# A gate's sigmoid computed as a tanh, and the gate inputs' loads moved from GpSimd's queue to SyncE's

## The chip, the cores and the metric

The kernel runs on one core of a Trainium2 chip. The metric is the device time of one execution in microseconds (us); the time before is 2019.53 us, the median of three runs (2018.4 to 2019.54). Lower is better.

## The reference

One layer of a streaming encoder is applied to a prompt of 1,024 frames and to 64 further frames of a running stream (1,088 tokens together), model width 2,048. An input projection gives the columns of two branches. The first, a state-space branch of width 1,024, ends in a gated linear unit (GLU), and this is the part that the change touches:

```
zs    = gelu(y_ssm)
y_ssm = zs * sigmoid(zs @ w_glu + b_glu)
y_ssm = y_ssm * silu(z_ssm)
y_ssm = rmsnorm(y_ssm, ssm_ng)
```

The second is an attention branch with 8 heads of width 128: q and k are RMS-normalised, forget gates are added to the logits, and then come a softmax, the product with v, and a SiLU gate. Both branches are normalised, concatenated, multiplied by `w_out` and added to the input. The outputs are the new frames, the new rows of k, v and the forget gates, and the final states.

## The kernel before

Everything is transposed: a tile has 128 features on the partitions and the 1,088 tokens along the free axis, in three blocks of 384, 384 and 320 columns (`COLS`), each block in a PSUM bank of its own (`GB`).

**The weight stream.** All large products run through the class `Weights`. A weight piece is two 128x128 tiles. SyncE loads it (`load`, L166, into one of four slots of `wraw`), ScalarE rounds it to its high part (`split_hi`, L171, `whi`), VectorE takes the rest (`split_lo`, L175, `wlo`), and TensorE multiplies (`multiply`, L187): 3 blocks x 2 tiles x 3 products = 18 matmuls. Piece m is split four pieces ahead of its use, into the slots of the piece m-4, which must have been multiplied; and SyncE may load piece m once piece m-4 has been split by VectorE. Each engine has one instruction stream, written out step by step; a step s is one piece.

**The stages.** A state-space stage comes first, and then eight attention heads (`part(h, True, ...)`, 32 pieces each). In the steps of head h lies also the softmax of head h-1. `part(None, False, True, NH - 1)` is the GLU stage: 32 pieces of `w_glu` in 8 panels of 4 pieces (`GP` is 4), and between them the softmax of the last head, in 9 row blocks. At the steps in `S_AT` (0, 3, 5, 7, 10, ...) logits are made, and ScalarE runs an Exp over them (L1522), which VectorE scales (L1726, tile `PR`). At the steps in `T_AT` (2, 4, 6, 8, 12, ...) TensorE transposes the result (L1986, L1989 for the 64-row block), behind the 18 matmuls of that step. At those in `O_AT` (3, 5, 7, ...) it multiplies with V (L1944). 128 pieces of `w_out` follow.

**One panel of the GLU.** When step 4n+3 is multiplied, ScalarE makes three Sigmoids from the three PSUM banks into `SG` (L1473), with the bias in a column of `vec`. The next panel's first matmuls wait for the bank they write. At the head of step 4n+4 VectorE runs `gate_glu(n)` (L1610): `SG` times `ZG` (L1614), then times `ZS` (L1616). ScalarE squares the product later in the same step (`square_glu`, L1435), behind `split_hi` and the step's copy of transposed rows, and VectorE adds the squares up (L1650, L1653). `SG`, `QG`, `ZG` are the buffers `QR`, `KR`, `VR` of the heads, and `ZS` lies in `KO`, the buffer from which the last head's k rows are stored.

**Table sets.** Some of ScalarE's functions need a table set that must be loaded first. `table(func)` (L1427) runs a one-column activation of that function, so that its set is loaded there: the trace shows an `ACT_TABLE_LOAD` and a small `ACTIVATE`. In the GLU stage `table(ACT.Sigmoid)` stands at the end of step 4n+2 (L1560), `table(ACT.Exp)` right behind the three Sigmoids (L1475).

**Who loads the gate inputs.** GpSimd, in its own stream (L1374 to L1381). For panel 0 it waits until the last head's v is transposed (`v_mm`) and its k rows are stored from `KO` (`k_out`); for the panels after, it waits for the product of the panel before (`yg`), stores it to `ys_s` (`finish_glu`, L1373), and loads `ZG` and `ZS` of the next. SyncE's stream in that stage has the weight pieces (`glu_piece`), the reload of the attention outputs (`load_ya`, L1284), and then the pieces of `w_out` with the reload of the gated products (`load_ys`, L1289).

Of the kernel before, what the change touches and what calls it, by code (L numbers as in the profile page):

```python
# [23 lines left out]
NH, HD = 8, 128  # L24
# [3 lines left out]
P = 128  # L28
# [8 lines left out]
RAW, SPL = 4, 4  # L37
# [13 lines left out]
def build_kernel(nc, x_prompt, x_sample, cache_k, cache_v, cache_logf, state_ssm_re, state_ssm_im,  # L51
# [66 lines left out]
    with ctx:  # L118
# [14 lines left out]
        def group(bank, b, p=slice(0, P)):  # L133

            return bank[p, 512 * b:512 * b + COLS[b][1]]

        def cols(a, b):

            return a[:, COLS[b][0]:COLS[b][0] + COLS[b][1]]
# [1012 lines left out]
        def attention(st, W, past):  # L1152
# [33 lines left out]
            stands = {}  # L1186
# [76 lines left out]
            def sync(sp, state_space):  # L1263
                def head(h, s):
                    col = h * P + 2 * D_SSM + D_ATT * (s // 8)
                    W.load(sp, h * NPC + s, s, col, PIECE * (s % 8))
                for s in range(NPC):
                    head(0, s)
                    state_space(s)
                with sp.Fori(1, NH) as h:  # L1270
                    for s in range(NPC):
                        head(h, s)

                def glu_piece(s):
                    W.load(sp, GLU0 + s, s, s // GP * P, PIECE * (s % GP), w_glu_v)

                def load_z(k):
                    sp.wait_ge(W.mm, W.multiplied(GLU0 - NPC // 4 + k // PIECE))
                    sp.dma_start(raw(XL[:, k]), zg_s[k * P:(k + 1) * P, :]).then_inc(zin[k], 16)

                def load_ya(k):
                    sp.wait_ge(W.mm, W.multiplied(GLU0 - NPC // 4 + (KG + k) // PIECE))
                    sp.wait_ge(e["y_out"], 16 * (k + 1))
                    sp.dma_start(raw(XL[:, KG + k]), ya_s[k * P:(k + 1) * P, :]).then_inc(yain[k], 16)  # L1284

                def load_ys(k):
                    sp.wait_ge(W.mm, W.multiplied(OUT0 - GP + k // PIECE))
                    sp.wait_ge(e["ys_out"], 16 * (k + 1))
                    sp.dma_start(raw(XL[:, k]), ys_s[k * P:(k + 1) * P, :]).then_inc(ysin[k], 16)  # L1289

                def out_load(n, s):
                    W.load(sp, out_piece(n, s), s, n * P, out_k(s), w_out_v, apart=s == HPC)
                for s in range(RAW):
                    glu_piece(s)
                    for k in range(PIECE * s, PIECE * (s + 1)):
                        load_z(k)
                for s in range(RAW, KG * GP):
                    glu_piece(s)
                    if s - RAW < KG - 1:
                        load_ya(s - RAW)  # L1300
                for s in range(NPO):
                    out_load(0, s)
                    if s >= HPC:
                        for k in range(PIECE * (s - HPC), min(PIECE * (s - HPC + 1), KG - 1)):
                            load_ys(k)
                with sp.Fori(1, NCH) as n:
                    for s in range(NPO):
                        out_load(n, s)
                stand(sp, "load")
                c = (NCH - 1) * P  # L1310
                for i in range(2):
                    sp.wait_ge(f["add"], stands["add"] + 2 * (NCH - 1) + i + 1)
                    sp.dma_start(y_prompt[0].rearrange("(m p) n -> p m n", p=P)[:, 4 * i:4 * i + 4, c:c + P], XO[1][:, 4 * i:4 * i + 4]
                                 ).then_inc(f["end_out"], 16)
                sp.wait_ge(f["add"], stands["add"] + 2 * (NCH - 1) + 3)
                sp.dma_start(y_sample[0][:, c:c + P], XO[1][0:DEC, TT - 1]).then_inc(f["end_out"], 16)
                sp.wait_ge(f["end_out"], 48)

            def gpsimd(pool):
# [52 lines left out]
                    pool.wait_ge(e["yg"], stands["yg"] + n + 1)  # L1372
                    pool.dma_start(ys_s[n * P:(n + 1) * P, :], SG[:]).then_inc(e["ys_out"], 16)  # L1373
                for n in range(KG):  # L1374
                    if n == 0:
                        pool.wait_ge(e["v_mm"], NH)
                        pool.wait_ge(e["k_out"], 32 * NH)
                    else:
                        finish_glu(n - 1)
                    pool.dma_start(ZG[:], zg_s[n * P:(n + 1) * P, :]).then_inc(e["zs_in"], 16)  # L1380
                    pool.dma_start(ZS, zs_s[n * P:(n + 1) * P, :]).then_inc(e["zs_in"], 16)  # L1381
                part(None, False, True, NH - 1)
                pool.wait_ge(e["v_out"], 32 * NH)

# [37 lines left out]
            def scalar(act, tail):  # L1422
# [35 lines left out]
                def part(h, gemm, att, ha):  # L1458
                    last = isinstance(h, int) and h == NH - 1
                    for s in range(NPC):  # L1460
# [3 lines left out]
                        if not gemm and s % GP == GP - 1:  # L1464
                            n = s // GP
                            if n:
                                act.wait_ge(e["ys_out"], 16 * n)
                            for b in range(3):
                                if b < 2:
                                    act.wait_ge(W.done[b], W.tiles + 4 * NH + n + 1)  # L1470
                                else:
                                    act.wait_ge(W.mm, W.multiplied(NH * NPC + s))
                                S.activation(cols(SG, b), group(GB, b), ACT.Sigmoid, bias=vec[:, 8 + n:9 + n]  # L1473
                                             ).then_inc(e["sig"], 1)
                            table(ACT.Exp)  # L1475
                        if gemm and s in (7, 15, 23):
                            raw = {7: QR, 15: KR, 23: VR}[s]
                            if s == 7 and att:
# [77 lines left out]
                            S.copy(KO[0:DEC, TT - 1], TB[0:DEC, 4 * 512:4 * 512 + P]).then_inc(e["k_act"], 1)  # L1556
                        if not gemm and s in YA_AT:
                            split_ya(YA_AT[s])
                        if not gemm and s % GP == GP - 2:
                            table(ACT.Sigmoid)  # L1560
                        if not gemm and s % GP == 0 and s:
                            square_glu(s // GP - 1)
                        if gemm and s == NPC - 2:
# [43 lines left out]
            def vector(dve, tail):  # L1607
                o = Order(dve, "dve_att")

                def gate_glu(n):  # L1610

                    dve.wait_ge(e["sig"], stands["sig"] + 3 * n + 3)
                    dve.wait_ge(e["zs_in"], 32 * (n + 1))
                    V.tensor_tensor(SG[:], SG[:], ZG[:], ALU.mult).then_inc(e["y1"], 1)  # L1614
                    dve.wait_ge(e["y1"], stands["y1"] + n + 1)
                    V.tensor_tensor(SG[:], SG[:], ZS, ALU.mult).then_inc(e["yg"], 1)  # L1616

                def gates(s):

# [49 lines left out]
                def part(h, gemm, att, ha):  # L1669
                    last = isinstance(h, int) and h == NH - 1  # L1670
                    for s in range(NPC):
# [11 lines left out]
                        if gemm:  # L1683
                            m = s + SPL
                            W.split_lo(h * NPC + m, m)
                            if not att:
                                tail(s)
                                if s == 6:
                                    state_space_over(dve)
                                    V.tensor_scalar(qg[:], vec[:, 32:33], HD ** -0.5, None, ALU.mult).then_inc(e["qg"], 1)  # L1690
                                    dve.wait_ge(e["qg"], 1)
                            if not att:
                                gates(s)
                        else:
                            W.split_lo(NH * NPC + s + SPL, s + SPL)
# [472 lines left out]
```

## Time and profile before

| what | value |
|---|---|
| median of three runs | 2019.53 us |
| the profiled execution's own time | 2019.47 us |
| its span | 2017.9 us |
| TensorE busy (matmuls) | 1965.8 us, 97% |
| VectorE busy | 1019.1 us, 51% |
| ScalarE busy | 681.3 us, 34% |
| GpSimd busy | 463.3 us, 23% |
| mean granted TensorE clock | 0.993 of full speed |
| mean DMA rate over the span | 89 GB/s |

The span runs from the first to the last instruction of the profiled execution. The time of an execution is a little longer: 1.6 us lie around the span. The matmuls are pipelined, so that the durations of two neighbours overlap; a busy share near 100% says that TensorE had always something to do, not that it was at its peak. Bracketed text at the end of a timeline row tells how long the engine was idle before it, and what released it.

### The profile page before, as it was taken

The page shows a single profiled execution, that of the slowest core. Times are in us where ns is not written, and L with a number is a line of the kernel's source. Part 1 is how long each engine was busy: PE and PEld are TensorE (multiplying, and loading weights), DVE is VectorE, ACT ScalarE, POOL GpSimd, SP SyncE. Part 2 cuts the span into 40 slices and gives each one's busy share as a digit, 9 for nine tenths or more (in the row PEclk, how much of TensorE's full clock was granted, in tenths as well). Part 3 has the DMA queues.
Part 4 walks back from the last instruction along what each step waited for, and adds up shares of the span by engine and source line. Part 5 has one row for each costly group of instructions (what it writes and reads, how often), then busy time and mean ns, then how long its engine had stood idle before and what let it go on. Part 6 is the DMA issues. An engine that isn't in the chain of part 4 may idle for free.

```text
span 2017.9 us, 35512 instructions
## 1 busy us (share of the span) xinstructions
PE 1965.8 (97%) x12368; PEld 1901.7 (94%) x12368; DVE 1019.1 (51%) x1984; ACT 681.3 (34%) x1368; POOL 463.3 (23%) x732
## 2 busy tenths in 40 slices
PE   5999999999999999999999999999989999999999
PEld 4799999999999999999999999999988999999998
DVE  7755666555453544635445354544655643333333
ACT  6422333333333343343333433343456631111110
POOL 5864444555110010010100001010020212222221
PEclk8999999999999999999999999999999999999999
DMA  8344444344322121131311213121273533333332
GB/s 226 95 107 109 108 111 104 104 115 129 86 57 62 35 82 37 34 85 31 84 34 45 73 34 84 34 78 39 82 254 132 201 93 86 86 86 86 88 86 65
DMA packets 220264, 179.91 MB, mean 89 GB/s; under 512 B 33090, under 2 KB 200156, under 8 KB 218996
## 3 DMA queue, kind: packets, MB, share of 16 engines
q1 hardware_dynamic: 200032, 117.39, 22.4%
q0 software_dynamic: 14656, 50.71, 8.1%
q10 hardware_dynamic: 5524, 11.14, 1.5%
q8 instruction: 30, 0.49, 0.1%
q14 instruction: 22, 0.18, 0.0%
HBM read 133.24 MB, written 45.93 MB: 89 GB/s over the span
## 4 chain that ended last, share of the span: by engine, by line
PE 89%; DVE 5%; ACT 2%; issue 2%; DMA 2%; SPq 0%; POOL 0%; DVEq 0%; ACTq 0%; POOLq 0%
PE GB L187 64%; PE TB L187 9%; PE TB L1944 3%; PE TB L1965 3%; PE TB L1986 2%; PE TB L1126 1%; PE TB L1136 1%; PE TB L1137 1%; PE TB L2005 1%; PE TB L2045 1%; PE TB L1032 1%; PE GB L1048 1%; DVE XL L668 1%; PE TB L1930 1%; ACT L1427 0%
## 5 line engine op out<-in xcount | busy, mean ns | idle before, releaser
L187 PE MATMUL GB<-XH,whi 128*128 128x384 f32 x2832 | 955.9, 338 | 10.3 <-DVE UP L744 5.1
L187 PE MATMUL GB<-XH,wlo 128*128 128x384 f32 x2832 | 926.6, 327 | 0.0
L187 PE MATMUL GB<-XL,whi 128*128 128x384 f32 x2832 | 923.7, 326 | 0.0
L175 DVE TENSOR_TENSOR wlo<-wraw,whi 128x256 fp32r<-128x256 f32 x540 | 269.8, 502 | 711.6 <-ACT whi L171 707.3
L187 PEld LDWEIGHTS GB<-XH,whi 128*128 128x128 f32 x2832 | 532.4, 188 | 26.2 <-issue 13.2
L187 PEld LDWEIGHTS GB<-XL,whi 128*128 128x128 f32 x2832 | 532.7, 188 | 5.3 <-issue 3.8
L171 ACT CAST whi<-wraw 128x256 fp32r<-128x256 f32 x540 | 218.3, 406 | 943.1 <-PE GB L187 785.2
L187 PEld LDWEIGHTS GB<-XH,wlo 128*128 128x128 f32 x2832 | 531.7, 188 | 0.0
L1341 POOL DMA_DIRECT2D ya_s<-ZR x7 | 4.1, 587 | 729.6 <-DVE ZR L1703 729.6
L1750 DVE RECIPROCAL SQ<-SQ 128x136 f32<-128x136 f32 x128 | 127.6, 997 | 1.1
L187 PE MATMUL TB<-XH,wlo 128*128 128x384 f32 (+1 forms) x384 | 125.8, 328 | 0.0
L187 PE MATMUL TB<-XH,whi 128*128 128x384 f32 (+1 forms) x384 | 125.5, 327 | 0.0
L187 PE MATMUL TB<-XL,whi 128*128 128x384 f32 (+1 forms) x384 | 125.5, 327 | 0.0
L1522 ACT ACTIVATE PR<-PR,nmx 128x128 f32<-128x128 f32 (+8 forms) x72 | 53.4, 742 | 186.5 <-DVE nmx L1721 173.3
L1427 ACT ACT_TABLE_LOAD x64 | 82.1, 1283 | 1.1
L1944 PE MATMUL TB<-PT,VT 128*128 128x128 f32 x576 | 74.7, 275 | 0.8 <-ACT PT L1532 0.8
L1944 PEld LDWEIGHTS TB<-PT,VT 128*128 128x128 f32 x576 | 71.3, 191 | 1.6 <-ACT PT L1532 1.3
L1965 PE MATMUL TB<-KN,QN 128*128 128x512 f32 (+2 forms) x192 | 72.4, 486 | 0.0
L187 PEld LDWEIGHTS TB<-XH,whi 128*128 128x128 f32 x384 | 72.1, 188 | 0.1
L187 PEld LDWEIGHTS TB<-XH,wlo 128*128 128x128 f32 x384 | 72.1, 188 | 0.0
L187 PEld LDWEIGHTS TB<-XL,whi 128*128 128x128 f32 x384 | 72.0, 188 | 0.0
L1716 DVE CUSTOM_DVE_ANT_0 PR<-TB,NCB 128x128 f32<-128x128 f32 (+3 forms) x64 | 41.0, 640 | 33.4 <-PE TB L1965 22.2
(389 smaller groups left out, 2060.3 us busy)
## 6 DMA issues: line engine op xcount, KB each, us to landing
wraw<-in_w_in SPq DMA_DIRECT2D x380, 128.0 KB, 2.2
wraw<-in_w_out SPq DMA_DIRECT2D x128, 128.0 KB, 2.2
xt<-in_x_prompt SPq DMA_DIRECT2D x5, 1024.0 KB, 5.5
NCB<-nc_s POOLq DMA_DIRECT2D x8, 608.0 KB, 5.2
us_s<-UP SPq DMA_DIRECT2D x8, 548.0 KB, 2.9
U<-us_s SPq DMA_DIRECT2D x64, 68.5 KB, 3.0
vs_s<-SS SPq DMA_DIRECT2D x8, 548.0 KB, 2.7
YT<-vs_s SPq DMA_DIRECT2D x64, 68.5 KB, 2.8
```

The costliest lines, as they stand in the source:

```text
L171: S.copy(whi[:, s % SPL], wraw[:, s % RAW]).then_inc(self.hi, 1)
L175: V.tensor_tensor(wlo[:, s % SPL], wraw[:, s % RAW], whi[:, s % SPL].bitcast(f32), ALU.subtract).then_inc(self.lo, 1)
L187: ins = T.matmul(group(GB if bank is None else bank, b), w[:, s % SPL, kk], x[:, k + kk, c:c + n], start=first and kk == 0 and i == 0, sto ...
L668: V.tensor_tensor(XL[:, 4 * b:4 * b + 4, m * P:m * P + n], tb, XH[:, 4 * b:4 * b + 4, m * P:m * P + n].bitcast(f32), ALU.subtract).then_in ...
L1032: ins = T.matmul(TB[0:2 * NH, 4 * 512:4 * 512 + n], wg[:, k], x[:, k, c:c + n], start=k == 0 and x is XH, stop=k == KT - 1 and x is XL)
L1427: o.then(S.activation(tabs[:], epsc[:], func))
L1522: S.activation(PR[0:n, 0:w], PR[0:n, 0:w], ACT.Exp, bias=nmx[0:n], accum_out=rsum[0:n]).then_inc(e["exp"], 1)
L1716: V.tensor_tensor_reduce(out=PR[0:n, 0:w - n], in0=TB[0:n, 0:w - n], in1=NCB[0:n, c:c + w - n], scale=1.0, scalar=-3e38, op0=ALU.add, op1= ...
L1750: o.then(V.reciprocal(a, a))
L1944: ins = T.matmul(O, VT[:, b], PT[:, b * P:(b + 1) * P], start=b == 0, stop=b == i)
L1965: ins = T.matmul(TB[:, c:c + cw], q, KN[:, c:c + cw], start=True, stop=True)
L1986: ins = T.transpose(TB[:, 1024 + b * P:1024 + (b + 1) * P], PR[:, b * P:(b + 1) * P], ident[:])
```

## The change

Five edits, which make one version:

1. ScalarE computes tanh((x + b)/2), in place of sigmoid(x + b), by `ACT.Tanh` with `scale=0.5`; VectorE makes up for it in the two products, as sigmoid(t) = 0.5 (1 + tanh(t/2)): (SG + 1) * ZG, then (SG * 0.5) * ZS. Both become `scalar_tensor_tensor`.
2. Eight columns of `vec` (the bias `b_glu`) are halved once by VectorE, in the first head. ScalarE waits for that before the first panel.
3. `table(ACT.Sigmoid)` and `table(ACT.Exp)` of the GLU stage are left out.
4. The loads of `ZG` and `ZS` are issued by SyncE (`load_gate(n)`) behind weight piece 8+4n of the GLU, and for n = 6 and 7 behind pieces 0 and 4 of `w_out`, where n = 7 stands ahead of the first `load_ys`. The waits are those that GpSimd had.
5. GpSimd keeps only the stores to `ys_s`. ScalarE gets a wait on `sqg`, its own squaring of the panel before.

```diff
@@ sync
+                def load_gate(n):
+                    if n == 0:
+                        sp.wait_ge(e["v_mm"], NH)
+                        sp.wait_ge(e["k_out"], 32 * NH)
+                    else:
+                        sp.wait_ge(e["yg"], stands["yg"] + n)
+                    sp.dma_start(ZG[:], zg_s[n * P:(n + 1) * P, :]).then_inc(e["zs_in"], 16)
+                    sp.dma_start(ZS, zs_s[n * P:(n + 1) * P, :]).then_inc(e["zs_in"], 16)
+                AHEAD = RAW + SPL
                 for s in range(RAW, KG * GP):
                     glu_piece(s)
                     if s - RAW < KG - 1:
                         load_ya(s - RAW)
+                    if s >= AHEAD and (s - AHEAD) % GP == 0:
+                        load_gate((s - AHEAD) // GP)
                 for s in range(NPO):
                     out_load(0, s)
+                    if s % GP == 0 and s // GP < AHEAD // GP:
+                        load_gate(KG - AHEAD // GP + s // GP)
                     if s >= HPC:
                         for k in range(PIECE * (s - HPC), min(PIECE * (s - HPC + 1), KG - 1)):
                             load_ys(k)
@@ gpsimd
                 for n in range(KG):
-                    if n == 0:
-                        pool.wait_ge(e["v_mm"], NH)
-                        pool.wait_ge(e["k_out"], 32 * NH)
-                    else:
+                    if n:
                         finish_glu(n - 1)
-                    pool.dma_start(ZG[:], zg_s[n * P:(n + 1) * P, :]).then_inc(e["zs_in"], 16)
-                    pool.dma_start(ZS, zs_s[n * P:(n + 1) * P, :]).then_inc(e["zs_in"], 16)
@@ scalar
                             if n:
                                 act.wait_ge(e["ys_out"], 16 * n)
+                                act.wait_ge(e["sqg"], stands["sqg"] + n)
+                            else:
+                                act.wait_ge(e["qg"], 2)
...
-                                S.activation(cols(SG, b), group(GB, b), ACT.Sigmoid, bias=vec[:, 8 + n:9 + n]
+                                S.activation(cols(SG, b), group(GB, b), ACT.Tanh, bias=vec[:, 8 + n:9 + n], scale=0.5
                                              ).then_inc(e["sig"], 1)
-                            table(ACT.Exp)
...
-                        if not gemm and s % GP == GP - 2:
-                            table(ACT.Sigmoid)
@@ vector
-                    V.tensor_tensor(SG[:], SG[:], ZG[:], ALU.mult).then_inc(e["y1"], 1)
+                    V.scalar_tensor_tensor(SG[:], SG[:], 1.0, ZG[:], ALU.add, ALU.mult).then_inc(e["y1"], 1)
                     dve.wait_ge(e["y1"], stands["y1"] + n + 1)
-                    V.tensor_tensor(SG[:], SG[:], ZS, ALU.mult).then_inc(e["yg"], 1)
+                    V.scalar_tensor_tensor(SG[:], SG[:], 0.5, ZS, ALU.mult, ALU.mult).then_inc(e["yg"], 1)
...
-                                    dve.wait_ge(e["qg"], 1)
+                                    V.tensor_scalar(vec[:, 8:16], vec[:, 8:16], 0.5, None, ALU.mult).then_inc(e["qg"], 1)
+                                    dve.wait_ge(e["qg"], 2)
```

## Rows read from the trace of the kernel before

**Rows 1.** The page's head, and the GLU stage as one stretch by engine

```profile
span 2017.9 us, 35512 instructions
...
core 0: us, PE busy (x) PEld busy (x) DVE busy (x) ACT busy (x) POOL busy (x), PEclk, DMA share, GB/s
1476.00:1606.00 130.00, 119.01 (x725) 112.89 (x724) 70.33 (x147) 77.37 (x137) 18.96 (x30) 1.00 0.51 173
```

**Rows 2.** TensorE's waits from 1475 to 1640 us: total, times, longest

```profile
PE TB L1986 <- DVE PR L1726: 5.2, 2, 3.1
PE GB L187 <- ACT QR L1473: 3.8, 4, 1.7
...
PE TB L1989 <- DVE PR L1726: 1.2, 1, 1.2
PE TB L1944 <- ACT PT L1532: 0.8, 2, 0.5
```

**Rows 3.** Timeline of TensorE, steps 4 and 6 of the GLU

```profile
1494.45 0.44 PE L1986 MATMUL TB<-ident,PR 128*128 128x128 f32 x2 [2.07 <-DVE PR L1726]
...
1505.18 0.55 PE L1986 MATMUL TB<-ident,PR 128*128 128x128 f32 x3 [3.15 <-DVE PR L1726]
```

**Rows 4.** Timeline of ScalarE, panels 0 and 2

```profile
1489.40 1.28 ACT L1427 ACT_TABLE_LOAD   x1
...
1490.93 0.41 ACT L171 CAST whi<-wraw 128x256 fp32r<-128x256 f32 x1
...
1499.61 1.12 ACT L1435 ACTIVATE KR<-QR 128x1088 f32<-128x1088 f32 x1 [4.31 <-DVE QR L1616]
1500.63 0.39 ACT L171 CAST whi<-wraw 128x256 fp32r<-128x256 f32 x1
...
1524.62 1.28 ACT L1427 ACT_TABLE_LOAD   x1
...
1526.14 1.47 ACT L1473 ACTIVATE QR<-GB,vec 128x384 f32<-128x384 f32 x3
```

**Rows 5.** Timeline of VectorE around the first gate product

```profile
1494.04 0.35 DVE L1726 TENSOR_SCALAR PR<-PR,rrec 128x256 f32<-128x256 f32 x1
1496.95 1.29 DVE L1614 TENSOR_TENSOR QR<-QR,VR 128x1088 f32<-128x1088 f32 x1 [2.56 <-DMA KO<-zs_s]
```

**Rows 6.** The chain that ended last, two of its pieces: start, us, what

```profile
1481.18 8.14 DMA out_k_sample<-KO
...
1490.50 6.35 DMA KO<-zs_s
```

**Rows 7.** Timeline of SyncE: weight pieces 8 and 9, and a reload

```profile
1480.51 0.38 SPq L166 DMA_DIRECT2D wraw<-in_w_glu  x1
1480.99 0.56 SPq L1284 DMA_DIRECT2D XL<-ya_s  x1
1483.70 0.38 SPq L166 DMA_DIRECT2D wraw<-in_w_glu  x1
```

**Rows 8.** Loads of 544 KB by SyncE (L1279) and by GpSimd (L1381): issue and landing

```profile
L1279 SPq DMA_DIRECT2D XL<-zg_s x8: 430/444/471, 1449.0 to 1466.4; - x8
...
DMA to landing us min/median/max: 3.9/4.6/6.2
...
L1381 POOL DMA_DIRECT2D KO<-zs_s x8: 531/531/543, 1490.5 to 1598.3; - x8
...
DMA to landing us min/median/max: 6.4/7.9/9.0
```

**Rows 9.** Groups by line from 1484 to 1612 us: busy us, mean ns of one

```profile
L1427 ACT ACT_TABLE_LOAD x16 | 20.5, 1283 | 0.3
...
L1614 DVE TENSOR_TENSOR QR<-QR,VR 128x1088 f32<-128x1088 f32 x8 | 10.3, 1284 | 2.6 <-DMA KO<-zs_s 2.6
L1661 DVE SCALAR_TENSOR_TENSOR XL<-XL,vec,XH 128x1088 fp32r<-128x1088 f32 x7 | 9.4, 1348 | 1.4 <-ACT XH L1444 1.4
```

**Rows 10.** Timeline of ScalarE in the first head: the loads at its Exp and its Ln

```profile
549.00 1.28 ACT L1503 ACT_TABLE_LOAD   x1
...
552.72 1.28 ACT L1506 ACT_TABLE_LOAD   x1
```

**Rows 11.** The first reloads of the gated product, and the split that reads them

```profile
1597.88 2.47 SPq L1289 DMA_DIRECT2D XL<-ys_s  x2
...
1609.52 2.29 ACT L1452 ACTIVATE XH<-XL,vec 128x1088 fp32r<-128x1088 f32 x2
```

## The prediction

> **What bounds the kernel now.** I read the page's head, then the GLU stage as one stretch, then TensorE's waits there, and last the timelines of the other engines around the two longest waits. TensorE is the bound: over the whole span it is nearly always busy, and in the GLU stage it is busy 119.01 of 130.00 us at a granted clock of 1.00 [rows 1]. The change adds and removes no matmul. All that it can give is therefore in the 11.0 us in which TensorE stood still there, and the waits account for them: 5.2 + 3.8 + 1.2 + 0.8 = 11.0 us [rows 2]. Two come from the softmax's normalised rows being late for a transpose (2.07 us at step 4, 3.15 us at step 6 [rows 3]), one of 1.2 us from the same at step 8, four (3.8 us) from a PSUM bank that the Sigmoid had not yet emptied, and two (0.8 us) from a late copy of transposed rows. The reader should ask of each: is ScalarE late because of a table load, or because of the gate inputs?
>
> **The table loads (edits 1 and 3).** 16 loads of 1283 ns stand in the stage [rows 9]. With its one-column activation each costs 1490.93 - 1489.40 = 1.53 us from its start to the next instruction [rows 4]; without it ScalarE still needs about 0.04 us to go on, so I take 1.5 us. 24 us of ScalarE's time go, but ScalarE is not the bound, and only what ends in a TensorE wait counts.
>
> - Step 4. Behind panel 0's Sigmoids ScalarE loads the Exp set, and only then splits a weight piece at 1490.93. VectorE's split, its logits, the Exp and the scaling follow, up to 1494.39 [rows 5], and the transpose at 1494.45. Without that load all of it comes 1.5 us earlier (the load ahead of the Sigmoids doesn't count here, since their last bank comes from TensorE). Wait 2.07 -> 0.57 us.
> - Step 8 is the same chain: 1.2 us of wait, 1.5 us of load gone, so the whole 1.17 us.
> - Bank waits. At panel 2 the load begins at 1524.62, right behind the Exp of step 10, and the Sigmoids at 1526.14 [rows 4]. Without the load they begin 1.5 us earlier, which leaves about 0.2 us of the longest wait (1.7 us). The other three are together 3.8 - 1.7 = 2.1 us, each under 1.5 us, and go whole. Gain 1.5 + 2.1 = 3.6 us.
> - The two late copies, 0.8 us, stand behind the Exp load of their panel, and go.
>
> Without step 6 this is 1.17 + 3.6 + 0.8 = 5.55 us behind step 6, and 1.5 us ahead of it.
>
> A row against a rule: the Trainium skill ("ScalarE: Activation LUTs", What ACT_TABLE_LOAD costs) gives a switch 1283 ns for the load and some 1380 ns of drain more, 2.66 us in all. Here the load and all that goes with it take 1.53 us [rows 4], so that the drain is not seen, and the row decides. By the page step 4's wait would have gone whole, which makes the sum about 0.5 us larger at most.
>
> **The gate loads (edit 4).** The wait at step 6 has another cause. After 1494.39 VectorE stands 2.56 us for `ZS` [rows 5], which landed 6.35 us after its issue at 1490.50; and that issue had waited for the store of the last k rows, out of the same buffer, until 1481.18 + 8.14 = 1489.32 [rows 6]. Behind the gate product are queued, on ScalarE, the squaring at 1499.61 and behind it the split at 1500.63 [rows 4], and from that the row block which TensorE waits for at 1505.18 [rows 3]. So step 6's transpose comes 1505.18 - 1496.95 = 8.23 us after the start of the gate product. Without the table load VectorE would arrive there at 1494.39 - 1.5 = 1492.9 us, and would wait for the load even longer. What the removed table load gives at step 4 is given back at step 6, unless the load lands earlier.
>
> The store that must end is the same, and the data ahead of it in the queues is nearly the same. SyncE is there in time: it issues piece 8 at 1480.51 and a reload at 1480.99 [rows 7], and would then stand at `load_gate(0)` from about 1481.6 until 1489.3. GpSimd's second load was issued 1490.50 - 1489.32 = 1.2 us after the store had landed; SyncE's, with 0.44 us for one [rows 8], about 0.5 us after, at 1489.8. SyncE's own loads of the same shape land in 4.6 us in the median (3.9 to 6.2), GpSimd's in 7.9 (6.4 to 9.0) [rows 8]. Of these I take 4.6: it landed at 1494.4, I say 1494.5. Bounds: 6.2 gives 1496.0; at best the product begins when VectorE arrives, 1492.9 (the store could land sooner, as SyncE issues nothing meanwhile).
>
> The two products cost 1348 instead of 1284 ns each [rows 9], 0.12 us on this chain. Step 6's transpose then comes at 1494.5 + 8.23 + 0.12 = 1502.85, which is 2.33 us earlier than before. TensorE would be ready at 1494.45 - 1.5 + (1505.18 - 3.15 - 1494.45 = 7.58) = 1500.5, so 2.3 us of wait stay. At best the transpose comes at 1501.25, 3.9 us earlier; with 1496.0 it is 0.8 us.
>
> Panels 1 to 7. `load_gate(n)` waits for a product that VectorE makes just ahead of the split which lets SyncE issue the piece in front of it; so that wait is over when SyncE comes to it. The loads have then most of a panel (some 14 us) to land; even 9.0 us is hidden. Weight pieces behind a pair come up to a pair's landing later, but are split four steps after their issue (over 12 us); hidden too. If that cover were gone, each late microsecond would be one of TensorE's.
>
> **What is queued behind SyncE's new wait.** Piece 9 was issued at 1483.70 [rows 7]; now it stands behind the pair, at about 1490.3, and behind it piece 10 and two reloads. Piece 9 is split after the first squaring, at 1494.5 + 0.12 + (1500.63 - 1496.95 = 3.68) = 1498.3. That leaves 8.0 us to land, against 3.9 to 6.2 for 544 KB in the rows of SyncE, and 128 KB here. I take nothing; at the longest row, 9.0, it would be 1.0 us. The last pair stands ahead of the first two reloads of the gated product, which were issued at 1597.88 and are read at 1609.52 [rows 11]: the pair's two issues and its bytes take some 2 to 3 of those 11.6 us. Nothing, by the same reasoning.
>
> **The rest.** 16 products of +0.064 us are 1.0 us on VectorE, which is idle half the stage (70.33 of 130 us [rows 1]). The halving of eight columns and the wait behind it are small instructions on an engine with gaps, in the first head, and at most some 0.2 us. Tanh takes what Sigmoid did, as no row shows it; if it were dearer by half of three instructions (0.7 us of 1.47), each bank wait would come back in part, some 2 us in all.
>
> **The sum.** 2.33 (steps 4 and 6 together) + 1.17 + 1.5 + 2.1 + 0.8 = 7.9 us. The profiled execution took 2019.47 us, of which 1.6 us lie around its span [rows 1], and is as good as the median, 2019.53. 2019.5 - 7.9 = **2011.6 us**. Its own bounds: 3.9 in place of 2.33 gives 2010.0; 0.8 gives 2013.1; all of the 11.0 us, which nothing here reaches, 2008.5.
>
> **Rivals.**
>
> - *The move gives no earlier landing.* The store, the data and the 16 engines are the same; if a pair takes SyncE as long as it took GpSimd (6.35 us from the second issue), `ZS` lands at 1489.8 + 6.35 = 1496.2 and the sum is 5.55 + 0.6 = 6.2: 2013.3 us. For it speaks that both queues are in a busy stretch then; against it the gap between the two rows of landings. The Trainium skill ("DMA: Bandwidth & Descriptors", Rules for kernel authors) says that spreading loads over other issuing engines gives no bandwidth and saves only the sequencer's issue time; by it this rival is the likelier one. Here no row shows the same pair on both queues. Chance 0.22.
> - *Tanh isn't in the set that is loaded.* Then a load stands before each panel's first Tanh and another before the next Exp. Rows show that a set loaded for Exp does not serve everything: an Ln right behind an Exp loads again [rows 10]. But a set holds several functions: between two panels the square, the casts and the Exp run with no load but the two of L1427 [rows 4, 9]. No row has a Tanh. Each panel has then two loads of 1.28 us where it had two of 1.5, in much the same places, and gains 0.2 us per late chain, about 1.3 us in all; with the 2.33 us of the gate loads 2015.9 us. Chance 0.08. The Trainium skill ("ScalarE: Activation LUTs", Table sets: the hidden batching unit) lists tanh among the functions of the exp set, which speaks against this rival; no run here shows it yet.
> - *Slower: SyncE's queue starves TensorE.* SyncE stands for the store of k, and piece 9, the first weight behind it, is late. The place is step 5, where ScalarE splits it; the price is one for one, beyond 1498.3 us. It is already 1 us at a landing of 9.0 us; to lose all of the 7.9 us and 4 more, the piece would have to land at 1510, after 20 us. A store that ends late by that much, as the only wait, would do it. Nothing in the rows does: 0.04.
> - *The stage's waits move elsewhere.* TensorE reaches the copies, banks and the split of the reloaded product sooner, and some 3 to 5 us come back as new waits: 2015 to 2017 us. VectorE and ScalarE have room (70 and 77 minus 24 of 130 us [rows 1]), so 0.11.
>
> My own forecast has 0.55.
>
> **Range.** From 2009.0 (just under its best case, 2010.0) to 2016.5, which takes in the second and third cases and most of the last. Its own range is 2010.0 to 2013.5. A measurement of this kernel can tell about 0.2%, 4 us. Faster by over 0.2%: 0.55 + 0.22 and a few hundredths of the others, 0.80. Within 0.2%: 0.15. Slower: 0.05.
>
> **What would show it.** In the changed trace no ACT_TABLE_LOAD lies in the GLU stage; the span drops by 7.9 us, all between 1486 and 1606 us; the waits for the Sigmoids' banks fall from 3.8 to about 0.2 us, those at steps 4, 6 and 8 from 2.07, 3.15 and 1.17 to 0.6, 2.3 and 0; VectorE's wait for `KO<-zs_s` falls from 2.56 to some 1.6 us, as it comes 1.5 us sooner; SyncE shows a stand of some 7.7 us in front of the first gate load, with no one waiting for a weight. I am wrong if table loads stay, if the pair lands after 1496, or if a wait for piece 9 or for the reloads shows up.

## The result

The changed kernel takes 2008.58 us (median of six runs, 2005.79 to 2009.19), the kernel before 2018.93 us (six runs, 2017.84 to 2019.54, three of them those behind the 2019.53 us): ratio 0.9948, 95% interval 0.9938 to 0.9957, so 10.35 us faster. I had forecast faster, with 2011.6 us and a range down to 2009.0. The direction was right, and so were the places where time was to be won; but I had the cost of a stop of TensorE too low, and the time lies 0.4 us under the range. Measured twice more, on one chip each, the same kernel came to 0.9953 (0.9939 to 0.9966) and 0.9956 (0.9943 to 0.9969), 8.5 and 9.4 us between the medians.

### The profile page after: what moved, and what is told of

Same layout as the page of the kernel before. It is cut to its first block, busy times and chain, and to the rows that moved or that the text cites. A ratio compares the mean times of both kernels' runs of the same rounds, so it can differ in the third digit from the quotient of the medians.

```text
span 2007.5 us, 35481 instructions
## 1 busy us (share of the span) xinstructions
PE 1964.0 (98%) x12368; PEld 1901.6 (95%) x12368; DVE 1017.6 (51%) x1985; ACT 657.1 (33%) x1336; POOL 452.4 (23%) x716
## 4 chain that ended last, share of the span: by engine, by line
PE 92%; DVE 4%; DMA 1%; issue 1%; ACT 1%; SPq 0%; POOL 0%; DVEq 0%; ACTq 0%; POOLq 0%
PE GB L187 67%; PE TB L187 9%; PE TB L1954 3%; PE TB L1975 3%; PE TB L1996 2%; PE TB L1126 1%; PE TB L1136 1%; PE TB L1137 1%; PE TB L2015 1%; PE TB L2055 1%; PE TB L1032 1%; DVE XL L668 1%; PE GB L1048 1%; PE TB L1940 1%; DVE xt L660 0%
```

## The profile after

The span is 2007.5 us. The GLU stage by engine, as in [rows 1]:

```profile
1476.00:1606.00 130.00, 127.40 (x787) 122.44 (x786) 77.32 (x155) 60.11 (x114) 12.17 (x16) 1.00 0.59 201
```

TensorE's busy time in the same window rises from 119.01 to 127.40 us. This is all that is left of its waits, in the same view as [rows 2]:

```profile
PE TB L1996 <- DVE PR L1736: 2.5, 2, 2.2
PE GB L187 <- ACT SQ L1595: 1.4, 1, 1.4
```

The second line belongs to the output stage and stood there before (1.4 us, once). The bank waits, the late copies and step 8's wait are gone. The timeline of TensorE has the two stops that remain, which answer to [rows 3] (a stop is here a stretch in which TensorE stands idle):

```profile
1491.98 0.44 PE L1996 MATMUL TB<-ident,PR 128*128 128x128 f32 x2 [0.36 <-DVE PR L1736]
...
1501.74 0.55 PE L1996 MATMUL TB<-ident,PR 128*128 128x128 f32 x3 [2.18 <-DVE PR L1736]
```

On ScalarE (timeline, panels 0 and 2, against [rows 4]) the split of the weight stands directly behind the third Tanh, and in panel 2 the three Tanh directly behind the Exp:

```profile
1488.04 0.53 ACT L1485 ACTIVATE QR<-GB,vec 128x320 f32<-128x320 f32 x1 [0.29 <-PE GB L187]
1488.47 0.40 ACT L171 CAST whi<-wraw 128x256 fp32r<-128x256 f32 x1
...
1519.86 1.45 ACT L1485 ACTIVATE QR<-GB,vec 128x384 f32<-128x384 f32 x3
```

No load stands in the stage: the 64 loads of `table` over the whole span have become 48. By the Trainium skill ("ScalarE: Activation LUTs", Table sets: the hidden batching unit), tanh is in the exp set, and the trace agrees. Three Tanh take 1.45 us where three Sigmoids took 1.47. On SyncE (timeline, against [rows 7]) the two loads of the first pair, the piece behind them, and a stand of 7.5 us ahead, which nobody waited for:

```profile
1480.24 0.49 SPq L1284 DMA_DIRECT2D XL<-ya_s  x1
1488.30 0.33 SPq L1304 DMA_DIRECT2D VR<-zg_s  x1
1488.67 0.43 SPq L1305 DMA_DIRECT2D KO<-zs_s  x1
1489.15 0.42 SPq L166 DMA_DIRECT2D wraw<-in_w_glu  x1
```

And on VectorE (against [rows 5]) the first product, whose idle time ahead of it falls from 2.56 to 1.69 us:

```profile
1493.62 1.29 DVE L1623 SCALAR_TENSOR_TENSOR QR<-QR,VR 128x1088 f32<-128x1088 f32 x1 [1.69 <-DMA KO<-zs_s]
```

**A ruler for the stage.** Two profiles do not enter the stage at the same time, so I measure from its first matmul to the matmul behind the wait for `ACT SQ`, a little into the output stage. These rows of TensorE's timeline are of the kernel before:

```profile
1476.29 0.42 PE L187 MATMUL GB<-XH,whi 128*128 128x384 f32 x1
...
1639.79 0.41 PE L187 MATMUL GB<-XH,whi 128*128 128x384 f32 x1 [1.37 <-ACT SQ L1586]
```

and these of the changed one:

```profile
1475.54 0.41 PE L187 MATMUL GB<-XH,whi 128*128 128x384 f32 x1
...
1629.38 0.41 PE L187 MATMUL GB<-XH,whi 128*128 128x384 f32 x1 [1.37 <-ACT SQ L1595]
```

163.50 us before, 153.84 after: the stage gives 9.66 us. The other 0.75 us was there at its entry. All profiles by this ruler (the transposes counted from the entry):

| kernel | entry | transpose of step 4 | of step 6 | of step 8 | stage |
|---|---|---|---|---|---|
| before | 1476.29 | 18.16 | 28.89 | 37.88 | 163.50 |
| before, again (e5) | 1472.51 | 18.17 | 28.87 | 37.85 | 163.40 |
| changed | 1475.54 | 16.44 | 26.20 | 33.96 | 153.84 |
| changed, again (e3) | 1474.33 | 16.45 | 26.46 | 35.78 | 155.65 |
| changed, third (e9) | 1473.09 | 16.46 | 26.72 | 36.04 | 155.92 |
| Tanh alone (e1) | 1474.34 | 16.46 | 29.42 | 39.41 | 159.30 |
| Tanh alone, again (e11) | 1475.26 | 16.45 | 29.40 | 38.56 | 158.44 |
| move alone (e2) | 1474.38 | 18.17 | 26.53 | 35.51 | 161.08 |
| tables back (e6) | 1475.16 | 18.16 | 26.35 | 35.34 | 160.94 |
| pair behind piece 6 (e7) | 1473.89 | 18.62 | 28.14 | 35.90 | 155.77 |
| early first pair (e4) | 1475.66 | 16.46 | 25.04 | 32.80 | 152.67 |
| and late square (e8) | 1476.25 | 16.42 | 23.84 | 31.54 | 151.41 |
| the same, again (e10) | 1472.35 | 16.43 | 23.84 | 31.54 | 151.42 |

## The experiments

**e1 and e11: the Tanh without the move.** The changed kernel, with the gate loads in GpSimd's stream again:

```diff
-                    if s >= AHEAD and (s - AHEAD) % GP == 0:
-                        load_gate((s - AHEAD) // GP)
...
-                    if n:
+                    if n == 0:
+                        pool.wait_ge(e["v_mm"], NH)
+                        pool.wait_ge(e["k_out"], 32 * NH)
+                    else:
                         finish_glu(n - 1)
+                    pool.dma_start(ZG[:], zg_s[n * P:(n + 1) * P, :]).then_inc(e["zs_in"], 16)
+                    pool.dma_start(ZS, zs_s[n * P:(n + 1) * P, :]).then_inc(e["zs_in"], 16)
```

> Edits 1 to 3 alone: Tanh, the halved bias, no table loads in the GLU stage; the gate inputs are still loaded by GpSimd. Theory A (a stop of TensorE costs more than the idle time that its row shows, as that time is counted from the modelled end of the last matmul; and step 6 is set by the landing of the gate inputs): the transpose of step 4 comes 1.7 us earlier in the stage and that of step 6 at the same place as before, and all behind it gains 6.9 us; the time falls by about 6.9 us against the kernel before. Theory B (idle time as the rows show it is what a stop costs, as in the prediction): 5.5 us. Theory C (the gain came from the move of the loads): under 2 us.

Measured: 2011.88 us against 2018.15, ratio 0.9969 (0.9957 to 0.9981). Step 4 comes 1.7 us earlier, and step 6 gives it all back and 0.5 us more (29.42 against 28.89 us): VectorE waited 4.9 us for the pair. From step 8 to the end the stage takes 119.89 us, as in the changed kernel (119.88) and 5.73 less than before (125.62). That is what theory A says. But the stage as a whole gained only 4.2 us in this profile, not 6.9 (between the medians lie 6.3 us, with an interval of 3.8 to 8.7, so the times alone can't decide between theories A and B): TensorE stood still for 5.4 us at step 6, and behind it the stretch to step 8 took 9.99 us, where the changed kernel took 7.76. The view by windows shows why (the granted clock of TensorE stands third from the end of each row):

```profile
1500.00:1505.00 5.00, 1.24 (x5) 1.24 (x6) 2.96 (x12) 1.47 (x5) 0.13 (x1) 0.68 0.98 324
1505.00:1510.00 5.00, 5.00 (x23) 4.98 (x22) 0.00 (x0) 1.80 (x5) 0.00 (x0) 0.63 0.24 82
1510.00:1515.00 5.00, 5.00 (x32) 4.55 (x31) 3.66 (x12) 1.53 (x7) 0.00 (x0) 1.00 0.09 26
```

Here the clock fell inside the stop: microsecond by microsecond it is granted 0.92 from 1501 and 0.50 from 1502 on, while TensorE comes back only at 1503.76, and 1.00 again from 1509 on.

The second time:

> Edits 1 to 3 alone once more. Its stage lost 2.2 us at half the clock behind a stop of 5.4 us. Theory A (the longer the stop, the likelier the fall): from step 6's transpose to step 8's it takes 10.0 us again, where 7.8 are enough at full clock, stage 159.3 us. Rival (chance, whatever the stop): 7.8 us there, stage 157.1 us.

Measured: 2013.55 us against 2018.82, ratio 0.9975 (0.9961 to 0.9988). A stop of 5.37 us, and 9.16 us from step 6 to step 8, so 1.4 us of lost clock: the fall came again, with a smaller loss. Neither forecast was met exactly; theory A is nearer.

**e2: the move without the Tanh.** The kernel before, with SyncE's and GpSimd's part of the change (the first two parts of the diff under "The change").

> Edits 4 and 5 alone: SyncE loads the gate inputs; Sigmoid and both table loads per panel stay. Theory A (only the first pair matters, and it lands about 2.5 us earlier than GpSimd's): the transpose of step 6 comes 2.3 to 2.7 us earlier, nothing else moves, the time falls by about 2.6 us. Rival (the move saves only issue time): 0.6 us. Rival (SyncE's stand costs weights): slower than before.

Measured: 2015.13 us against 2018.15, ratio 0.9985 (0.9976 to 0.9994), 3.0 us. In the stage step 6 comes 2.36 us earlier and nothing else moves (stage minus 2.42 us). TensorE's waits:

```profile
PE GB L187 <- ACT QR L1481: 3.8, 4, 1.7
PE TB L1994 <- DVE PR L1734: 2.9, 2, 2.1
...
PE TB L1997 <- DVE PR L1734: 1.2, 1, 1.2
PE TB L1952 <- ACT PT L1540: 0.8, 2, 0.5
```

Only the line of `PR` has changed against [rows 2], from 5.2 to 2.9 us. VectorE's wait for `KO<-zs_s` is 0.2 us, as it comes to the product some 1.7 us later than with the Tanh. So the move saves more than the 0.7 us of issue time, and SyncE's stand costs nothing. The Trainium skill ("DMA: Bandwidth & Descriptors", Rules for kernel authors) has it that another issuing engine saves only issue time; on bandwidth no run here contradicts it, but in the changed kernel VectorE's product starts 4.95 us behind the issue of the second load (1488.67 to 1493.62), where it was 6.45 us before (1490.50 to 1496.95 [rows 5, 6]).

Whether those 1.5 us come from the queue is not shown. There is a rival that no run here separates: SyncE, while it stands for the store, issues no reload and no weight, so the pair starts on DMA engines with little else to do. These windows hold the moment just ahead of the first load's issue in the kernel before (1489.92), and the issue in the changed one (1488.30); the last two figures are the share of the DMA engines and the GB/s:

```profile
1489.00:1490.00 1.00, 1.00 (x7) 0.95 (x7) 0.00 (x0) 0.98 (x2) 0.08 (x1) 1.00 1.05 404
...
1488.00:1489.00 1.00, 1.00 (x8) 0.95 (x7) 0.10 (x1) 0.82 (x2) 0.00 (x0) 1.00 0.06 26
```

Over all eight panels `ZS` landed in 6.1 us in the median (4.8 to 7.8) from SyncE in the changed kernel, and in 7.9 (6.4 to 9.0 [rows 8]) from GpSimd; the other traffic differed there too.

**e3 and e9: the changed kernel again.** No edit.

> The changed kernel once more, on the same chip as its two halves. From the first matmul of the GLU stage to the end of the stage it gains 9.6 us as before; the time falls by 9.6 us, and what was measured beyond that (10.35 us) was chance in the prologue. If the two halves don't overlap, their gains add up to this one (6.9 + 2.6).

> The changed kernel a third time, beside the version with the early pair and the late square on the same chip. Its stage was 153.84 us once and 155.65 the second time, where the granted clock had fallen to half behind step 6's stop of 2.41 us. Theory A (that fall comes in some executions and not in others, when the stop is long): the stage is 153.8 or 155.6 us. Rival (the fall has nothing to do with the stop): it shows elsewhere, or in the version without that stop too.

Measured: 2009.63 us against 2018.15, and 2009.44 against 2018.82. The two halves, 6.3 us (e1) and 3.0 us (e2) between medians, add up to 9.3 us where the whole gave 8.5 on the same chip; the intervals, some 1.8 to 2.7 us to either side, don't tell these apart. The stages are 155.65 and 155.92 us. Up to step 6 they are as the first (26.46 and 26.72 against 26.20), behind step 8 too (119.87 and 119.88); from step 6 to step 8 they take 9.32 us against 7.76. Timeline of TensorE in e3, the weight piece behind step 6's stop:

```profile
1500.79 0.55 PE L1996 MATMUL TB<-ident,PR 128*128 128x128 f32 x3 [2.41 <-DVE PR L1736]
...
1501.52 0.34 PE L187 MATMUL GB<-XH,wlo 128*128 128x384 f32 x1
1501.70 0.47 PE L187 MATMUL GB<-XH,whi 128*128 128x384 f32 x1
...
1502.61 0.52 PE L187 MATMUL GB<-XH,whi 128*128 128x384 f32 x1
1502.93 0.52 PE L187 MATMUL GB<-XL,whi 128*128 128x384 f32 x1
```

A matmul of 384 columns starts every 0.32 us instead of every 0.17, and the window from 1500 to 1505 has a granted clock of 0.67: half the clock (1.2 of 2.4 GHz) for some 3.3 us, which costs 1.56 us. So the expectation of 9.6 us in the stage was wrong for two of three profiled executions, in which it was 7.9 and 7.6. Theory A of e9 fits: its 155.92 us is near the slower of the two figures that it named, and e10, without that stop, shows no fall.

**e5: the kernel before again.** No edit.

> The kernel before, profiled a second time. The changed kernel entered the GLU stage 0.75 us earlier than the kernel before, though nothing that it does ahead of that stage but two small instructions differs; three of its variants entered it at 1474.3 us. Theory A (chance of the prologue, where the granted clock was 0.92 in the first 150 us of the one and 0.97 to 0.98 of the others): this profile enters the stage anywhere from 1474.3 to 1476.3, and its stage takes 163.5 us as before. Theory B (the change makes the part ahead faster): it enters at 1476.3 again.

Its stage is the same (163.40 us), its entry 3.8 us earlier, and its span 2014.0 us against 2017.9. Theory B is refuted, and chance in the prologue is shown; it is larger than theory A had it, as this entry, 1472.51 us, lies ahead of the 1474.3 to 1476.3 that I had named. The entries of all profiles lie between 1472.35 and 1476.29 us, of kernels with and without the change alike.

**e6: the table loads back, the rest kept.**

```diff
                                 S.activation(cols(SG, b), group(GB, b), ACT.Tanh, ...
                                              ).then_inc(e["sig"], 1)
+                            table(ACT.Exp)
...
+                        if not gemm and s % GP == GP - 2:
+                            table(ACT.Silu)
```

> The changed kernel with its Tanh and its products, but with the table loads back in their old places: a one-column Silu at the end of step 4n+2 and a one-column Exp right behind the three Tanh. Theory A (the gain behind step 6 is the loads', whatever ScalarE and VectorE compute): stage as with the move alone, 161.1 us, 7.2 us more than the changed kernel's 153.8; TensorE's waits come back with 3.8, 1.2 and 0.8 us (5.8 in all), and the time lost at steps 8 and behind is 7.0 us, 0.16 us more for each of the seven stops. Rival (a stop costs just its idle time): 5.8 us there. Rival (Tanh and the products of two operations are cheaper or dearer themselves): another stage time than 161.1.

Measured: 2016.16 us, ratio 0.9996 (0.9987 to 1.0006), stage 160.94 us. The interval overlaps with that of the move alone (0.9976 to 0.9994), and the stages, 160.94 and 161.08 us, say that Tanh and its two products cost what Sigmoid and its own did. TensorE's waits:

```profile
PE GB L187 <- ACT QR L1485: 3.8, 4, 1.7
...
PE TB L2002 <- DVE PR L1739: 1.2, 1, 1.2
PE TB L1957 <- ACT PT L1544: 0.8, 2, 0.5
```

These are the same 5.8 us of idle time as in the kernel before, in the seven stops behind step 6. The stretch behind step 6's transpose takes 134.59 us here and 127.64 in the changed kernel: 6.95 us for 5.8 us of shown idle time. A stop costs 0.16 us more than its row says, in the mean (step 8's less: 1.23 us for the 1.17 shown). Steps 4 to 6 say the same of single stops. With no stop at step 6 they take 7.42 us (e8, e10: 7.41); with one they take the idle time of its row and 7.57 to 7.60 us (all the others but e7, which lost clock there), 0.15 to 0.18 us more. The timeline of the kernel before shows where they hide, ahead of the stop at step 4:

```profile
1491.92 0.31 PE L187 MATMUL GB<-XL,whi 128*128 128x320 f32 x1
1492.07 0.31 PE L187 MATMUL GB<-XH,wlo 128*128 128x320 f32 x1
1494.45 0.44 PE L1986 MATMUL TB<-ident,PR 128*128 128x128 f32 x2 [2.07 <-DVE PR L1726]
```

Two matmuls start 0.15 us apart and each is drawn 0.31 us long. The idle time counts from the modelled end, 1492.38; without the wait the next would have started at 1492.22.

**e7: the first pair two pieces earlier in SyncE's queue.**

```diff
+                    if s == AHEAD - 2:
+                        load_gate(0)
-                    if s >= AHEAD and (s - AHEAD) % GP == 0:
+                    if s > AHEAD and (s - AHEAD) % GP == 0:
```

> The changed kernel with the first pair of gate loads behind weight piece 6 in SyncE's stream, in place of piece 8; the other seven stay. SyncE then stands from about 1477 us until the last k rows are stored (1488), and piece 7 comes behind. Theory A (the rival of the prediction, once made true: weights starve): piece 7 is issued at 1489 in place of 1477, lands some 5 us later, behind the pair, and ScalarE splits it at 1494 in place of 1488.5; step 4's transpose comes 5 us later, step 6's about 4 us, the stage takes 158 us (perhaps 1 to 2 us more if the granted clock falls after the longer stop). Rival (there is slack also here, since a piece is loaded four steps ahead): 153.8 us.

Measured: 2009.82 us, ratio 0.9961 (0.9945 to 0.9976); stage 155.77 us, 1.93 more than the changed kernel's first profile, not 4. Step 4 comes 2.18 us later, and some 1.6 us are clock lost behind its stop of 2.53 us: from step 4 to step 6 it takes 9.52 us, where 7.42 and the 0.38 us of stop at step 6 with its 0.16 would be 7.96. In return the stop at step 6 is 1.8 us shorter (0.38 against 2.18 us). ScalarE does starve for piece 7 (timeline):

```profile
1488.99 0.41 ACT L171 CAST whi<-wraw 128x256 fp32r<-128x256 f32 x1 [2.06 <-DMA wraw<-in_w_glu]
```

It waits only 2.06 us, since the store of the k rows was over much sooner: SyncE's first load begins 9.7 us behind the entry of the stage (1483.63 - 1473.89), where in the changed kernel it is 12.8 (1488.30 - 1475.54). SyncE issued two reloads less ahead of it, and the store of the last 32 KB of k landed in 4.8 us, where it took 7.7 in the changed kernel. So the rival of my prediction is real, its price is about one for one (2.06 us of ScalarE's wait, 2.18 us at step 4), and my expectation of 158 us left out that a silent SyncE ends its own wait sooner.

**e4: the first pair without waiting for the store.** `ZS` of panel 0 goes into `SQ`:

```diff
-                        sp.wait_ge(e["k_out"], 32 * NH)
+                        sp.wait_ge(e["sqa"], NH - 1)
                     else:
+                        if n == 1:
+                            sp.wait_ge(e["k_out"], 32 * NH)
                         sp.wait_ge(e["yg"], stands["yg"] + n)
...
-                    sp.dma_start(ZS, zs_s[n * P:(n + 1) * P, :]).then_inc(e["zs_in"], 16)
+                    sp.dma_start(ZS if n else SQ[:], zs_s[n * P:(n + 1) * P, :]).then_inc(e["zs_in"], 16)
...
-                    V.scalar_tensor_tensor(SG[:], SG[:], 0.5, ZS, ALU.mult, ALU.mult).then_inc(e["yg"], 1)
+                    V.scalar_tensor_tensor(SG[:], SG[:], 0.5, ZS if n else SQ[:], ALU.mult, ALU.mult).then_inc(e["yg"], 1)
```

> The changed kernel with the first panel's second gate input in the buffer SQ, free at that point, in place of the one from which the last head's k rows are still being stored; SyncE doesn't wait for that store until the second pair. Theory A (the rest of the wait at step 6 hangs on the landing of the first pair, 1.7 us after VectorE arrives): the gate product starts as soon as VectorE comes to it, step 6's wait falls from 2.2 to about 0.5 us, 1.7 us less than the changed kernel. Rival (the wait at step 6 is set by the chain of ScalarE and VectorE behind step 5 anyway): no change.

Measured: 2008.15 us, ratio 0.9941 (0.9928 to 0.9955). Step 6 comes 1.16 us earlier than in the changed kernel, not 1.7, and its stop is 0.98 us, not 0.5. The missing 0.5 us is the pair's: it was issued seven microseconds earlier, at 1481, and still landed 0.5 us too late, as its `ZS` took 11.0 us to land, in the stretch in which stores, reloads and weights are all under way.

**e8 and e10: and the square later.** On top of e4:

```diff
-                        if not gemm and s % GP == 0 and s:
+                        if not gemm and (s % GP == 0 and s > GP or s == GP + 1):
                             square_glu(s // GP - 1)
...
-                        if not gemm and s % GP == 1 and s > 1:
+                        if not gemm and (s % GP == 1 and s > GP + 1 or s == GP + 2):
                             add_squares(s // GP - 1)
```

> The kernel with the early first pair, and besides it panel 0's square and its copy into the sum each one step later (ScalarE's at the end of step 5, VectorE's at step 6), so that the split of piece 9 no longer stands behind the square. Theory A (step 6's transpose hangs on gate product, square, split, in that order): the rest of its wait (1.0 us) goes, and only step 4's 0.4 us stays; stage 151.5 us, 1.2 us less than with the early pair alone. Rival (VectorE's own queue, with the two products ahead of the split, is what is late): at most 0.3 us less.

> The version with the early first pair and the late square once more. Theory A: no stop over 0.5 us in the stage, no fall of the granted clock, stage 151.4 us again; its time is 2.4 us under the changed kernel's, and up to 4 where that one loses clock. Rival (the 1.3 us over the early pair alone were chance): 152.7 us.

Measured: 2006.46 and 2006.54 us, ratios 0.9943 (0.9929 to 0.9956) and 0.9939 (0.9926 to 0.9952); stages 151.41 and 151.42 us. Step 6's stop is gone, as forecast, and neither profile has a fall of the clock in the stage (nor has e4's, with its stop of 0.98 us). The rivals of both expectations are refuted. Beside the changed kernel on the same chip (2009.44 us) it is 2.9 us faster by the medians, whose intervals overlap; by the stage it is 2.4 to 4.5 us. By the ruler it is the fastest version of all. TensorE's waits from the entry of the stage on, in e8:

```profile
PE GB L187 <- ACT SQ L1597: 1.4, 1, 1.4
PE TB L1998 <- DVE PR L1738: 0.4, 1, 0.4
```

## Why the prediction was right, and where it was wrong

The places of the gain and what causes each wait were right. The step that failed is the reading of idle time as the price of a stop: it made the terms for step 8 and behind it (1.17 + 1.5 + 2.1 + 0.8 us) 1.4 us too small, and with them the fast end of the range.

- *That only TensorE's 11.0 us of waits can be won, and that table loads and the first gate pair are behind them:* right. The two halves part as foreseen: e1 gives nothing up to step 6 and 5.7 us behind step 8, e2 gives 2.4 us at step 6 alone.
- *Step 4:* 1.5 us forecast, 1.72 measured, 0.36 of the 2.07 us of wait stays. I had left ScalarE 0.04 us to go on without the load; in fact the split starts 0.10 us before the row of the third Tanh ends (1488.04 + 0.53 - 1488.47). By the drain that the Trainium skill adds to a load ("ScalarE: Activation LUTs", What ACT_TABLE_LOAD costs) it would have gone whole; the measurement decides for the row. *Steps 4 and 6 together:* 2.33 forecast, 2.69 measured (28.89 to 26.20). The pair landed, counted from the entry, 0.1 to 0.2 us sooner than I had taken (1493.62 - 1475.54 = 18.08 us against 1494.5 - 1476.29 = 18.21), and a product of two operations with a constant took 1.29 us, what the plain product took, and not the 1348 ns of the row that I had put for it. The stop at step 6 is 2.18 us, forecast 2.3.
- *Step 8 and all behind it:* 1.17 + 1.5 + 2.1 + 0.8 = 5.6 us forecast, 1.23 + 5.74 = 6.97 us measured. This is the mis-sized term, and the failed step. I had read the idle times of the rows as what the stops cost. The seven stops that vanish cost 0.16 us more each in the mean, 1.15 us, as e6 shows by bringing them back; most of the rest is the 0.2 us of bank wait that I had left in.
- Together 2.69 + 6.97 = 9.66 us where the sum said 7.9. My bounds at the fast end were built on the same reading. The range ended at 2009.0 us, short even of the 2008.5 that "all of the 11.0 us" gave, and that is itself no bound when stops cost more than they show.
- *The base:* I had set the sum against 2019.5 us, an execution which entered the stage late by up to 4 us of chance (e5). The median beside the change was 2018.93. So the forecast of 2011.6 missed 2008.58 by 3.0 us: 1.8 in the stage, 0.6 by the base, and 0.7 between the 9.66 us of the stage and the 10.35 of the medians, which I can't tell from chance (the entries differed by 0.75 us; measured again, the gain was 8.5 and 9.4 us).
- *The clock:* the prediction had no term for it. A stop of 2.4 to 2.7 us at step 6 was followed by half clock in two of three profiles of the changed kernel, 1.56 us each. The first profile has no such fall, so it plays no part in that miss. Where it fell, the stage gained 7.9 and 7.6 us, near my 7.9 by luck alone: a cost that I had left out beside a gain that I had sized too small.
- *SyncE's stand:* forecast 7.7 us with no one waiting, measured 7.5, and no weight late. VectorE's wait: forecast 1.6, measured 1.69.
- *Rivals:* an equally late landing (0.22) is refuted by e2, though not for a reason that is shown (queue or free DMA engines); a load for Tanh (0.08) is refuted by the trace, and so are new waits elsewhere (0.11), as none shows between 1475 and 1640 us. The starving queue is real two pieces earlier in the queue (e7), and its price is one for one as the prediction had it; only the lateness was less than I had expected for e7.

What stays open: why the granted clock falls behind some stops and not behind others. It fell with stops of 2.41, 2.53, 2.66, 5.37 and 5.39 us, not behind those of 2.07 and 2.18, but also not in either profile of the kernel before, where 3.15 and 3.12 us of stop at step 6 followed on 2.07 us at step 4. No run here separates the length of a stop from what lay around it. Open too is why the pair lands sooner when SyncE loads it.

## What to carry to other kernels

Remove a table load by its place and not by its count: here 16 loads of 1.5 us gave 7 us, and the one ahead of a late transfer gave nothing until that transfer was moved as well. When matmuls overlap in the trace, a stop costs its idle time and the part of the last matmul's modelled duration in which the next would have run (here 0.16 us); check the sum against start-to-start times of undisturbed steps. Compare two profiles from a common event just ahead of the change, because the part in front of it may have moved by chance as much as the change gives.

## What the runs showed of the hardware

- TensorE's granted clock fell to half for some 3.3 us right behind a stop of 2.41 us (e3), between two stretches at full clock, and for some 6.8 us from inside a stop of 5.39 us (e1). Over five such stops the loss beyond the stop was 1.4 to 2.2 us. It did not fall with stops of 3.15 and 3.12 us in the two profiles of the kernel before.
- The prologue of one and the same kernel differed by 3.8 us from profile to profile (entries 1476.29 and 1472.51 of the kernel before), with a granted clock over the first 150 us of 0.92 and 0.94. That clock doesn't account for the entries: it was 0.98 with an entry of 1475.54 (the changed kernel) and 0.95 with one of 1472.35 (e10).
- In e4 the first `ZS`, a load of 544 KB, took 11.0 us when it was issued among the stores and reloads at 1481 us; the seven others of that run took 4.9 to 8.0 us. And a store of 32 KB landed in 4.8 us instead of 7.7 when SyncE issued two reloads and two weight pieces less beside it (e7).
- ScalarE's Tanh ran without a load of its own between Exps: 64 loads of `table` became 48, and three Tanh took 1.45 us where three Sigmoids took 1.47.
